# Order of the third mixture's experts, its row gather, and the adds of the first attention, on one Trainium2 core

## The reference

```python
def hier_moe(x, ...):                       # layers 1 and 2: D_EXPERT = 512
    g_idx = argmax(x @ w_grp_router + b)    # 1 of 4 groups
    top_v, top_i = top_k(e_logits[group], 2)        # 2 of its 8 experts
    gate = g_p * softmax(top_v)
    # each token row goes to its 2 experts, in blocks per expert
    h = silu(xb @ w_gate[e]) * (xb @ w_up[e])
    out[tok] += (h @ w_down[e]) * weight

def hierarchical_moe(t, ...):               # layer 3: D_EXPERT_2 = 256
    y = sum over experts of ((silu(t @ w_gate[e]) * (t @ w_up[e])) * combine) @ w_down[e]
    # combine is nonzero for 2 experts of each token
```

## Time and profile before

| | us |
|---|---|
| median of 3 runs | 2207.31 |
| the runs | 2206.63 to 2207.64 |
| span of the profiled execution (its own time 2207.31) | 2205.4 |
| PE busy | 2012.4 |
| DVE busy | 673.9 |
| attention steps with `project_heads` | 261 to 338 |
| experts of mixtures 0, 1, 2 | 410 to 891, 1071 to 1553, 1910 to 2176 |

### The profile page before, as it was taken

The page is one execution under the profiler, slowest core; times in us unless marked ns, Lnnn a source line. Parts: engine busy times, 40 slices in busy tenths (PEclk is TensorE's granted clock), DMA queues, the critical chain, the costliest instruction groups (busy, mean ns, idle before and its releaser), DMA issues.

```text
span 2205.4 us, 25848 instructions
## 1 busy us (share of the span) xinstructions
PE 2012.4 (91%) x10093; PEld 1067.4 (48%) x10093; DVE 673.9 (31%) x1584; ACT 404.6 (18%) x873; POOL 120.7 (5%) x148
## 2 busy tenths in 40 slices
PE   8999878999999999599999999999599989988873
PEld 4444434654554554554554554554454445644442
DVE  0154526411111111534411111111637224612113
ACT  1033413111111111121211111111223222112112
POOL 0000000100000000000100000000010001301100
PEclk9999988999999999799999999999799999999997
DMA  9931101699999999821699999999821110699995
GB/s 314 304 132 39 39 0 61 228 419 421 420 420 421 421 420 411 302 82 55 225 419 420 421 421 421 421 421 407 299 82 39 39 38 23 212 381 420 420 420 233
DMA packets 134625, 611.43 MB, mean 277 GB/s; under 512 B 15087, under 2 KB 53375, under 8 KB 71583
## 3 DMA queue, kind: packets, MB, share of 16 engines
q1 hardware_dynamic: 120735, 579.07, 66.3%
q0 software_dynamic: 13824, 31.48, 4.2%
HBM read 574.53 MB, written 48.55 MB: 283 GB/s over the span
## 4 chain that ended last, share of the span: by engine, by line
PE 82%; DMA 7%; DVE 6%; ACT 2%; issue 1%; POOL 0%; SPq 0%; POOLq 0%; ACTq 0%; DVEq 0%
PE bank L817 20%; PE bank L844 12%; PE bank L802 12%; PE bank L562 10%; DMA ring<-in_w_up_dram 5%; PE bank L702 4%; PE bank L574 4%; PE bank L548 3%; PE bank L826 3%; PE bank L656 2%; PE bank L1002 1%; PE bank L793 1%; PE bank L963 1%; PE bank L616 1%; PE bank L629 1%
## 5 line engine op out<-in xcount | busy, mean ns | idle before, releaser
L817 PE MATMUL bank<-ring,work 128*64 128x512 f32 x2048 | 450.7, 592 | 0.6 <-ACT work L1123 0.6
L1598 DVE TENSOR_TENSOR work<-work,bank 64x512 f32<-64x512 f32 (+1 forms) x96 | 87.0, 907 | 790.5 <-ACT work L1133 790.4
L844 PE MATMUL bank<-ring,work 128*64 128x512 f32 x1280 | 297.5, 603 | 3.6
L817 PEld LDWEIGHTS bank<-ring,work 128*64 128x64 f32 x2048 | 146.4, 137 | 291.6 <-issue 290.7
L802 PEld LDWEIGHTS bank<-work 128*128 128x128 f32 x2112 | 245.7, 191 | 57.1 <-issue 52.7
L802 PE MATMUL bank<-work 128*128 128x128 f32 x2112 | 270.8, 281 | 0.0
L562 PE MATMUL bank<-hT,ring 128*128 128x512 f32 x512 | 237.1, 606 | 0.7 <-ACT work L1065 0.7
L1138 ACT ACTIVATE work<-bank 64x512 f32<-64x512 f32 x96 | 56.7, 590 | 608.4 <-PE bank L844 608.4
L844 PEld LDWEIGHTS bank<-ring,work 128*64 128x64 f32 x1280 | 83.4, 137 | 146.1 <-issue 128.8
L562 PEld LDWEIGHTS bank<-hT,ring 128*128 128x128 f32 x512 | 94.0, 194 | 109.5 <-issue 107.6
L1133 ACT ACTIVATE work<-bank 64x512 f32<-64x512 f32 (+1 forms) x96 | 49.8, 518 | 441.6 <-PE bank L817 356.0
(11 more groups left out here) (291 smaller groups left out, 1747.7 us busy)
## 6 DMA issues: line engine op xcount, KB each, us to landing
ring<-in_moe_w_gate_dram SPq DMA_DIRECT2D x128, 1024.0 KB, 15.3
ring<-in_moe_w_up_dram SPq DMA_DIRECT2D x128, 1024.0 KB, 17.2
ring<-in_moe_w_down_dram SPq DMA_DIRECT2D x128, 1024.0 KB, 15.3
ring<-in_w_gate_dram SPq DMA_DIRECT2D x32, 1024.0 KB, 19.8
ring<-in_w_up_dram SPq DMA_DIRECT2D x32, 1024.0 KB, 21.9
ring<-in_w_down_dram SPq DMA_DIRECT2D x32, 1024.0 KB, 21.6
x_rows<-zeros SPq DMA_DIRECT2D x1, 12800.0 KB, 62.1
ring<-in_attn_w_qkv_dram SPq DMA_DIRECT2D x12, 1024.0 KB, 13.7
```

The costliest lines, as they stand in the source:

```text
L817: mm = pe.matmul(GU[BLK * a:BLK * a + BLK, :], xT_[:, 4 * kk + k, :], v[:, k, :], start=(kk + k == 0), stop=(kk + k == 4))
L844: mm = pe.matmul(DN[BLK * n:BLK * n + BLK, :], hT_[:, 2 * kk + k, :], v[:, k, 512 * n:512 * n + 512], start=(kk + k == 0), stop=(2 * kk + ...
L1598: dve.tensor_tensor(dealt(hg[:, 0:F], F // P), as_dealt(sg[:, 0:F], F // P), as_dealt(GU[BLK:P, 0:F], F // P), ALU.mult).then_inc(b.hg, 1)
```

## The change

Five parts.

**1. Order of layer 3's experts.** `over_slots` takes the place of `over_blocks` for l == 2. In the slot of expert j, PE issues gate and up of expert j + 1, then the turning of expert j's product, the row preparation (`ahead2`), and down of expert j. There are two gate/up banks (`GU2`) and two buffers each of `sg` and `hg`. SP loads in that order too: gate and up of j + 1, then down of j.

**2. Rows of layer 3.** POOL stores each tile of token rows once its norm is written, each row twice in a row, to `x_rows` (4 plain DMAs), which now has 1024 rows. Pairs 0 to 3 are picked by matmul with `sel`. For pairs 4 to 15, POOL gathers the rows from `x_rows` by `y_row`, skipping empty slots (`gather_rows`). The zero fill, `rows_of` and the 8 scatters are gone, as is a load for a pair 16 that does not exist.

**3. Routing arithmetic, all mixtures.** The slot numbers (`idx`) are signalled as soon as they are there. The overflow numbers and the token weights are computed after the first expert's DVE work. For l == 2 the whole chain stands behind expert 0's product and a copy.

**4. Attention adds.** `add_heads(step - 32)` stands at the head of DVE's step. Before it was `add_heads(step - 33)` at its end.

**5. Ends of stages.** SP waits for the stores itself and not for POOL (`load_tiles`). The last operation of `tile_normal` and `tile_rms` is done in two halves, each signalled; PE turns, or SP stores, a half at a time. `combine_tile(l, 1, 0)` stands behind the first tile's norm.

```diff
+                def load2(i, v, src):
+                    u = m.base + v
+                    sp.wait_ge(units_used, u - UNITS + 1 + UNITS * i)
+                    sp.dma_start(ring[u % UNITS][:, :], src).then_inc(unit_loaded[u % UNITS], 16)
+                def slot(i, s):
+                    gate, up, down = (a.rearrange("e (p k) n -> e p k n", p=P) for a in expert_weights)
+                    if not last_slot(i, s):
+                        load2(i, 3 * s + 2, gate[TURN * i + s + 1])
+                        load2(i, 3 * s + 3, up[TURN * i + s + 1])
+                    load2(i, 3 * s + (2 if last_slot(i, s) else 4), down[TURN * i + s])
...
-            sp.dma_start(x_rows.rearrange("(p n) (q c) -> p (n q) c", p=P, c=256),
-                         zeros[:, :].unsqueeze(1).to_broadcast([P, rows_ // P * 4, 256])).then_inc(rows_zeroed, 16)
...
+            def load_tiles(l):
+                sp.wait_ge(over_moved, l + 1)
+                for y_stored in steps.y_stored:
+                    sp.wait_ge(y_stored, 16 * (E // 4) * (l + 1))
+                for tt in range(T):
+                    rows = y_rows[2 * P * tt:2 * P * tt + 2 * P, :].rearrange("(p k) d -> p (k d)", k=2)
+                    sp.dma_start(ytile[tt], rows).then_inc(routing.gathered[tt], 16)
...
+                def ahead2(i, s):
+                    c, half = (s + 3) // 2, (s + 1) % 2
+                    if type(i) is int and 2 * i + c < 4:
+                        if half == 0:
+                            pe.wait_ge(main.sel, main.sel0 + c + 2 * i)
+                        turn_rows(main, c % 2, half, P)
+                        return
+                    if half == 0:
+                        pe.wait_ge(xg_loaded[c % 2], 16 * (c // 2 - 1) + 16 * i)
+                    for k in range(4):
+                        c0 = P * (4 * half + k)
+                        mm = pe.transpose(XT[half][:, P * k:P * k + P], xg[c % 2][:, c0:c0 + P], ident)
+                    mm.then_inc(main.xt, 1)
+                def slot(i, s):
+                    j = TURN * i + s
+                    if not last_slot(i, s):
+                        gate_up2(i, s + 1)
+                    pe.wait_ge(main.hg, main.n0 + j + 1)
+                    for k in range(half_f):
+                        mm = turn_block(k, HT[:, BLK * k:BLK * k + BLK], hg2[s % 2][:, P * k:P * k + P],
+                                        ident[BLK:P, BLK:P])
+                    mm.then_inc(main.ht, 1)
+                    if type(i) is not int or j < E - 3:
+                        ahead2(i, s)
+                    if type(i) is int and j == 3:
+                        turn_slots()
+                    pe.wait_ge(main.hT, main.n0 + j + 1)
+                    if type(i) is not int or j:
+                        pe.wait_ge(main.ysb, main.n0 + j)
+                    v = unit2(i, 3 * s + (2 if last_slot(i, s) else 4)).rearrange("p (k n) -> p k n", k=2)
+                    for k in range(2):
+                        for n in range(2):
+                            mm = pe.matmul(DN[BLK * n:BLK * n + BLK, :],
+                                           hgT[:, P * k // 2:P * k // 2 + BLK], v[:, k, 512 * n:512 * n + 512],
+                                           start=(k == 0), stop=(k == half_f - 1))
+                    mm.then_inc(main.used, 1)
...
+                def slot(i, s):
+                    if not last_slot(i, s):
+                        product2(i, s + 1)
+                    act.wait_ge(main.used, main.base + 3 * TURN * i + 3 * s + (3 if last_slot(i, s) else 5))
+                    if s % 2 == 0:
+                        act.wait_ge(main.y_stored[s // 2], main.store0 + 16 * i)
+                    rows = slice(BLK * (s % 2), BLK * (s % 2) + BLK)
+                    act.activation(ysb[s // 2][rows, 0:512], DN[0:BLK, :], ACT.Copy)
+                    act.activation(ysb[s // 2][rows, 512:D], DN[BLK:P, :], ACT.Copy).then_inc(main.ysb, 1)
...
-                dve.scalar_tensor_tensor(out=h[:, tt, :], in0=h[:, tt, :], scalar=rstd[:, tt:tt + 1],
-                                         in1=lnp[:, D:2 * D], op0=ALU.mult, op1=ALU.add).then_inc(done, 1)
-                dve.wait_ge(done, count0 + tt + 1)
+                for n in range(2):
+                    hs = h[:, tt, 512 * n:512 * n + 512]
+                    dve.scalar_tensor_tensor(out=hs, in0=hs, scalar=rstd[:, tt:tt + 1],
+                                             in1=lnp[:, D + 512 * n:D + 512 * n + 512], op0=ALU.mult, op1=ALU.add)\
+                        .then_inc(done, 1)
+                dve.wait_ge(done, count0 + 2 * tt + 2)
...
+                if step >= 32:
+                    add_heads(step - 32)
...
-                if step >= 33:
-                    add_heads(step - 33)
-            add_heads(7)
...
+                if l == 2:
+                    product2(0, 0)
+                    copy_rows(main, 1, 0, 3, P)
...
+                def slot(i, s):
+                    j, c, half = TURN * i + s, (s + 3) // 2, (s + 1) % 2
+                    dve.wait_ge(main.ht, main.n0 + j + 1)
+                    dve.tensor_copy(hgT[:, 0:F // 2], HT[:, 0:F // 2]).then_inc(main.hT, 1)
+                    if type(i) is not int or j < E - 3:
+                        copy_rows(main, c % 2, half, 2 * c + half + 1 + TURN * i, P)
+                    if not last_slot(i, s):
+                        product2(i, s + 1)
+                    if type(i) is int and j < 2:
+                        select(j % 2, 4 + 2 * j)
+                    if type(i) is int and j == 0:
+                        overflow_and_weights()
+                    if type(i) is int and j == 3:
+                        place_rows()
...
             tile_variance(0)
             for tt in range(T):
-                if tt + 1 < T:
+                if 1 <= tt < T - 1:
                     combine_tile(0, tt + 1, 0)
                 tile_normal(tt, 1, tiles_written, turns["ffn0"].src0)
                 if tt + 1 < T:
+                    if tt == 0:
+                        combine_tile(0, 1, 0)
                     combine_tile(0, tt + 1, 1)
                     tile_variance(tt + 1)
...
+                def gather_rows(q):
+                    if q >= 6:
                         pool.wait_ge(main.xt, main.x0 + 2 * (q - 1))
-                    pool.dma_start(xg[q % 2], x_rows[P * q:P * q + P, :]).then_inc(xg_loaded[q % 2], 16)
+                    pool.indirect_dma_start(
+                        out=xg[q % 2], out_offset=None, in_=x_rows,
+                        in_offset=bass.IndirectOffsetOnAxis(ap=y_row[:, q:q + 1], axis=0),
+                        bounds_check=2 * S - 1, oob_is_err=False).then_inc(xg_loaded[q % 2], 16)
...
+                        pool.wait_ge(tiles_written, turns["rms1"].src0 + tt + 1)
+                        pool.dma_start(x_rows[2 * P * tt:2 * P * tt + 2 * P, :].rearrange("(p k) d -> p k d", k=2),
+                                       hn[:, tt, :].unsqueeze(1).to_broadcast([P, 2, D])).then_inc(x_stored, 16)
...
+                    if l == 2 and 6 <= q + 4 < E // 2:
+                        gather_rows(q + 4)
```

241 lines of the change are left out of this document (129 added, 112 removed).

## The result

The changed kernel takes 2171.64 us, median of four runs, beside 2206.97 us: a ratio of 0.9847 (0.9827 to 0.9867). I had said 2160, in 2150 to 2177. On another chip, in five rounds, it was 0.9823 (0.9804 to 0.9842). The direction and the range hold, and the likeliest time was 12 us off. But 2171.64 lies outside the bounds that I gave the forecast itself, 2150 to 2166, and the sum behind it holds less well than the time.

A forecast was written before the change was run, and what follows sets the result against it. Transfers were taken to bind mixture 2, and waits for DVE's adds the end of the first attention. Savings of 24.0 + 20.7 + 3.1 = 47.8 us gave 2160 us, range 2150 to 2177, the forecast itself 2150 to 2166.

The forecast's parts named there:

- rival 1: Mixture 2: gathers cost as much as the loads did, giving 2168, up to 2172 us; chance 0.13.
- rival 2: Attention gives half, as DVE's 5.2 us do not fit PE's step or waits keep the low clock: 2172 us; chance 0.17.
- The low end: Forecast's lower bound, 2150 us: 26 from the attention, 6 us unused in mixture 2, shortest tail with 2.1 us more.
- Bound: Mixture 2: transfers at 420 GB/s bind, 8.43 us per expert against PE's own 7.38; PE doesn't become the bound after.
- Attention adds, -24.0: End of first attention: 14.67 us idle before six projections plus 9.74 us low-clock excess, less 0.4, go.
- the 0.4 I took off: First attention: deducted because the first add now stands ahead of step 32's maxima, which PE's next steps use.
- Mixture 2, bytes, -17.2: Mixture 2 to the last unit: 99.7 MB become 94.9, unused transfer time falls from 14.8 to 9 us.
- under 8 us each, and run off the 12 units already loaded: Mixture 2's first four slots, turning rows with 16 matmuls instead of 4, were claimed not to make PE the bound.
- Mixture 2, its end, -3.5: After the last gate and up of mixture 2: 8.8 us of remaining work before, 5.3 after.
- Ends, -3.1: Ends of mixtures 0, 1 and 2 and output in halves: 1.0 + 0.9 + 0.9 + 0.3 us saved, 0 to 4.
- Priced at nothing: Removed zero fill, early in the program, and mixtures 0 and 1 with their moved routing arithmetic: no change.
- Rival 3: Mixture 2: gather latency beyond 24 us holds PE and the ring, making it slower, 2240 us at 32 us; chance 0.03.

The follow-up runs named there:

- the two experiments: Attention adds alone moved in the kernel before: 2176.10 us beside 2203.98; adds put back in the changed kernel: 2194.42 us beside 2166.29 for the changed kernel.
- plain_loads: Changed kernel with each of the 12 gathers replaced by a plain load of 128 rows: 2172.18 us, ratio 0.9852 to the kernel before.
- no_pick: Changed kernel with rows of pairs 1 to 3 turned by 4 matmuls instead of picked with 16 (another result): ratio 0.9821 to the kernel before.
- after_again: The changed kernel once more, unaltered, on another chip: median 2166.29 us, ratio 0.9823 to the kernel before.
- down_first_last: Changed kernel with the old order for expert 30 alone, its down ahead of gate and up of expert 31: ratio 0.9840 to the kernel before.
- down_first_all: Changed kernel with down of j again ahead of gate and up of j + 1 throughout mixture 2: 2178.77 us, ratio 0.9893 to the kernel before.
- root_late: Changed kernel with ACT copying the first turned tile after mixture 0 before the second root: 2169.61 us, ratio 0.9821 to the kernel before.
- att_only: Kernel before with only the attention adds moved: 2176.10 us beside 2203.98, ratio 0.9867.
- after: The changed kernel's first profiled execution and runs: 2171.64 us beside 2206.97, ratio 0.9847.

## Why the prediction was right or wrong

**The time.** 2171.64 is in the range because the range took in rivals 1 and 2; the forecast had 2150 to 2166 for itself. Neither rival is what happened: the gathers were as small as I took them, and the attention gave more than forecast, not half. So that the time falls where those two stood is luck. The low end was also added up wrongly: its terms give 2153, not 2150.

**Bound.** Right for the middle of mixture 2: after about 2005 PE waits for up units, 24.8 us in all, and DMA is at 420. Wrong for its first third: there PE's slots bind. Rows 9 already had an expert at 7.38 us on PE in the first half of the kernel before, less than the 8.43 of the second half.

**Attention adds, -24.0.** Measured -26.2 in the profiled pair and 26 to 29 by the two experiments. The mechanism holds as told. The size was 2.2 us short. The low clock also held the work beside the projections (lost to the clock: 13.9 before, 3.2 after, 10.7 us, where I had 9.74 for the projections), and the 0.4 I took off was not seen; the other 0.8 I can't place. No projection waits, so rival 2 is out. That DVE's step is covered was a thin reading all the same: the 5.2 us end where the add starts and leave out its own 0.69.

**Mixture 2, bytes, -17.2.** Measured -12.6 to the last gate and up. The amounts were nearly right: 0.26 MB a gather, 100.3 and 94.4 MB where I had 99.7 and 94.9. `plain_loads` paid 6.9 us for 3.4 MB where I had 7.7 for 3.2, and rival 1 is out. What failed is the step "under 8 us each, and run off the 12 units already loaded". A picking is 3.84 us, there are six of them behind the first gate and up, and a slot is 9.5 us; the 12 units carry PE, but it is PE's pace that lets the next ones in. `no_pick` gives this step 6.0 us. In the changed kernel the scatters don't hold the stage either: without them nothing is gained. Whether they held the kernel before, as I read rows 7, no run shows. The unused time went from 13.3 to 15.4 us on my stretch where I had 14.8 and 9, and from 21.4 to 27.2 over the whole mixture.

**Mixture 2, its end, -3.5.** Measured +2.1. The mistake is the point from which I counted. I let the 8.8 us before run from the start of the last gate and up, and the 5.3 after from the landing of the last unit, as if the two fell together. They don't: before, the last unit lands 2.6 us behind that start, and ACT's last copy ends 6.2 us behind the landing; in `after_again` two units follow the last up, the last lands 4.9 us behind the start, and the copy ends 6.1 us behind it. So 5.3 was nearly right for what it named, and there was nothing to save. The one reordering tried at this end (`down_first_last`) gave nothing either.

**The order itself.** I named only the 0.63 us wait of one expert and called PE no bound. In the kernel before PE waited for the product 20.0 us in all (1900 to 2180; us in total, times, longest):

```profile
PE bank L793 <- DVE work L1598: 20.0, 30, 1.8
```

Against `down_first_all` the new order is worth 9.9 us, nearly as much as mixture 2 gained; but some 7 of these, by the estimate above, may belong to where that kernel prepares its rows. Fewer bytes without the new order gave nothing, and the new order with plain loads gave 3.6 (`plain_loads`, 260.5 beside 264.1). In these kernels fewer bytes and the new order gain together what neither gave by itself; the new order with the old bytes was not run.

**Ends, -3.1.** Stores to loads did what I said, 1.47 to 0.09 us at mixture 0. From it I took 0.4 for the moved combine, and it was nearly all of it: -0.1 at mixture 0, +0.6 at mixture 1, -1.9 at the end of the program instead of -1.2. At mixture 0 the cause is ACT's root ahead of the copy, as `root_late` shows. At mixture 1 I tried nothing; 1.0 us more is lost to the clock there.

**Priced at nothing.** The zero fill: the values' projection is 3.1 us shorter in the profiled pair, but `att_only`, which has the fill, also shows 55.9, and kernels without it show 57.4 to 57.8. So the 3.1 us are not the fill's. Mixtures 0 and 1: 0.8 and 1.4 us longer in that profile, 0 to 2 us in others, and I had named a longer one as a sign of being wrong. They too move 420 GB/s, so their lead is thin: PE waited 0.6 and 0.8 us for up units there, and for none before. I called them PE's own pace, which leaves this out.

**Rival 3** is out: no row of PE's waits names the gathered rows.

Taken together: 26.2 + 10.5 + 1.4 of the terms are 38.1 of the 47.8 predicted. The other stages, most of it the clock, gave 6.8 (start and way to mixture 0) and took 8.7 in the profiled pair, which leaves 36.2. That these two nearly cancel is chance as well.

## What to carry to other kernels

Where a stage runs off a ring of prefetched tiles, the pace of the first consumers sets how soon the refills start; cost each early slot from rows of the same instruction, and compare bytes freed per slot with the DMA rate, not only the middle of the loop. When a wait in an engine's list moves, list what stands behind it there: a square root ahead of a copy cost as much as a faster DMA hand-over gave. And cut both traces into stages before you believe a difference of medians: one stage here moved by 5 us and three more by 3 to 6 with no change in their instructions. When you undo a part of a change to price it, compare the result's list of instructions with the kernel before: the old order of one thing beside the new place of another is a third kernel.

## What the runs showed of the hardware

Identical instructions behind identical work got different clocks from one execution to the next: layer 3's attention took 159.2 to 159.7 us with 13.7 us lost to the clock, or 164.5 with 18.8. The values' projection took 55.9, about 57.6 or 58.9 us. The windows of before, `after` and `after_again` give a granted clock of 1.00 there, but the matmul records show where the time goes: the first seven took 1.06 to 1.19 us in the profile of before and the first four in `after_again`, where later ones take 0.59; in `after` none did. The Trainium skill (TensorE: Matmul & The Clock Gate, What's actually happening) says that the number of slow matmuls at a kernel's start varies from run to run and calls the ramp under 1% of a typical span; the 3 us here, 0.14% of the span, agree. The 5 us in layer 3's attention are a change of the granted clock in the middle of the program. An indirect gather that skips empty slots moved 0.26 MB where the plain load of the same tile moves 0.52. Beside ring loads at 420 GB/s the stores of 0.26 MB and the plain loads of 0.52 MB both landed in 8.0 to 8.3 us; the trace has no landing times for the gathers.
